# Attention probabilities turned by DMA transposes of their 16-bit halves instead of by TensorE

## The reference

```python
def dilated_group_attention(qb, kk, vv, rel_bias, window, dilation):
    ...
    s = jnp.einsum('brhnqd,brhnkd->brhnqk', qb.astype(jnp.float32), kk.astype(jnp.float32)) * scale + bias
    s = jnp.where(valid, s, NEG_INF)
    lse = jax.nn.logsumexp(s, axis=-1)
    p = jnp.exp(s - lse[..., None])
    o = jnp.einsum('brhnqk,brhnkd->brhnqd', p, vv.astype(jnp.float32))
    return o, lse

def mixer_b(xn, shared_kv, w_q, w_o, rel_bias):
    ...
    o = jnp.stack(outs, axis=0)
    lse = jnp.stack(lses, axis=0)
    wts = jax.nn.softmax(lse, axis=0)
    o = jnp.sum(wts[..., None] * o, axis=0)
    return o.reshape(b, s, D_MODEL).astype(xn.dtype) @ w_o
```

## Time and profile before

| | |
|---|---|
| median of 3 runs | 757.46 us (757.18 to 758.97) |
| the profiled execution | 759.1 us, its span 757.3 us |
| PE busy | 747.5 us, 99% of the span |
| DVE busy | 522.4 us, 69% |
| ACT busy | 420.9 us, 56% |
| POOL busy | 168.1 us, 22% |
| DMA | 144.87 MB, 191 GB/s over the span |

### The profile page before, as it was taken

One profiled execution on the slowest core, in us unless ns is written; L12 is line 12 of the kernel. 1 busy time (PEld: TensorE's weight loads), 2 busy tenths in 40 slices (PEclk: granted clock), 3 DMA queues, 4 the chain that ended last, 5 costly groups with the idle time before them and its releaser, 6 DMA issues.

```text
span 757.3 us, 13417 instructions
## 1 busy us (share of the span) xinstructions
PE 747.5 (99%) x4651; PEld 643.9 (85%) x4651; DVE 522.4 (69%) x738; ACT 420.9 (56%) x633; POOL 168.1 (22%) x298
## 2 busy tenths in 40 slices
PE   8999999999999999999999999999999999999996
PEld 7999988888888888999899898898888878888884
DVE  5788997876766657778666667568637675666653
ACT  3866667454343344866776766767746444433421
POOL 1000001225100000236656646674002000000000
PEclk9999999999999999999999999999999999999999
DMA  7745575599876575669687795696743987767602
GB/s 232 208 128 167 173 242 196 177 288 244 242 230 200 186 220 139 163 158 246 159 232 154 157 239 148 163 222 185 238 140 93 257 274 220 209 189 236 226 14 56
DMA packets 181571, 144.87 MB, mean 191 GB/s; under 512 B 29336, under 2 KB 170240, under 8 KB 181536
## 3 DMA queue, kind: packets, MB, share of 16 engines
q1 hardware_dynamic: 153344, 131.45, 55.9%
q0 software_dynamic: 6784, 7.41, 5.7%
q10 hardware_dynamic: 21408, 5.54, 5.0%
HBM read 138.02 MB, written 1.11 MB: 184 GB/s over the span
## 4 chain that ended last, share of the span: by engine, by line
PE 93%; DMA 2%; DVE 2%; issue 1%; ACT 1%; POOL 0%; DVEq 0%; POOLq 0%; SPq 0%; ACTq 0%
PE ps L1256 19%; PE ps L1257 19%; PE ps L1258 19%; PE ps L1504 10%; PE ps L1506 5%; PE ps L1262 3%; PE ps L1264 3%; PE ps L1263 3%; DMA work<-work 2%; PE ps L1567 1%; PE ps L1333 1%; PE ps L1350 1%; PE ps L1335 1%; PE ps L1336 1%; PE ps L1308 1%; PE ps L1532 1%
## 5 line engine op out<-in xcount | busy, mean ns | idle before, releaser
L841 DVE TENSOR_TENSOR w_lo<-raw,w_hi 128x2048 fp32r<-128x2048 f32 (+2 forms) x144 | 280.0, 1960 | 62.1 <-ACT w_hi L536 62.1
L536 ACT ACTIVATE w_hi<-raw 128x2048 fp32r<-128x2048 f32 (+2 forms) x144 | 233.2, 1638 | 81.5 <-DVE work L1085 29.8
L1256 PE MATMUL ps<-w_hi,xt 128*128 128x512 f32 x352 | 137.7, 391 | 0.0
L1258 PE MATMUL ps<-w_hi,xt 128*128 128x512 f32 x352 | 137.0, 389 | 0.0
L1257 PE MATMUL ps<-w_lo,xt 128*128 128x512 f32 x352 | 137.0, 389 | 0.0
L705 ACT ACTIVATE work<-ps,stat 128x256 f32<-128x256 f32 x44 | 21.0, 477 | 158.2 <-PE ps L1258 156.1
L445 POOL TENSOR_SCALAR stat<-stat 128x1 f32<-128x1 f32 x15 | 9.7, 648 | 407.4 <-ACT work L552 383.4
L1256 PE MATMUL ps<-w_hi,ot 128*128 128x512 f32 x240 | 94.9, 395 | 0.4 <-DVE ot L1106 0.4
L1257 PE MATMUL ps<-w_lo,ot 128*128 128x512 f32 x240 | 93.5, 390 | 0.0
L1258 PE MATMUL ps<-w_hi,ot 128*128 128x512 f32 x240 | 93.5, 390 | 0.0
L475 POOL DMA_DIRECT2D work<-bias_rows x128 | 71.4, 558 | 39.6 <-DVE ot L1106 25.8
(11 more groups left out here) (153 smaller groups left out, 1272.8 us busy)
## 6 DMA issues: line engine op xcount, KB each, us to landing
raw<-in_w_gate_up SPq DMA_DIRECT2D x88, 512.0 KB, 4.8
raw<-in_w_kv_b SPq DMA_DIRECT2D x96, 256.0 KB, 4.1
raw<-in_w_down SPq DMA_DIRECT2D x22, 1024.0 KB, 4.9
raw<-in_w_q_b SPq DMA_DIRECT2D x48, 256.0 KB, 4.6
raw<-in_w_qkv_a SPq DMA_DIRECT2D x23, 512.0 KB, 5.3
raw<-in_w_o_a SPq DMA_DIRECT2D x4, 1024.0 KB, 6.2
work<-bias_rows POOLq DMA_DIRECT2D x128, 32.0 KB, 3.6
raw<-in_w_o_b SPq DMA_DIRECT2D x4, 1024.0 KB, 7.0
```

The source lines that it names most:

```text
L536: act.activation(w_hi[:, s % CUT, 0:size(s)], raw[:, s % RAW, 0:size(s)], ACT.Copy).then_inc(hi_made, 1)
L841: dve.tensor_tensor(w_lo[:, c, 0:n], raw[:, s % RAW, 0:n], w_hi[:, c, 0:n].bitcast(F32), ALU.subtract).then_inc(lo_made, 1)
L1256: mm(out, xs[0], ws[0], start=start, stop=False)
L1258: return mm(out, xs[1], ws[0], start=False, stop=stop)
```

## The change

For pairs 0 to 6 TensorE no longer turns the probabilities. VectorE copies each head's block of 640 words of 32 bits apart into 1280 halves of 16 bits (`part_halves`), two DMA transposes issued by ScalarE turn them (`turn_halves`), and VectorE copies the turned halves together (`join_halves`). The second transpose is issued when the first has landed. There are three such buffers in place of two larger ones: `prob[0]`, `prob[1]` and `halves_in`. Probabilities now stand in five blocks of 128 columns, and two memsets a step clear the 64 columns that no key fills. The eighth pair is still turned by TensorE. To make room in `work`, the own band of the bias moves to the tile `ones` once that is free, and for the first two heads to `halves_in`. The diff without its lines on the eighth pair's calls and the semaphores:

```diff
@@ (layout of work)
-        TURNED = (P, P + SEQ, 0, 2 * SEQ)
-        turned = [carve(P + WS) for _ in range(2)]
-        prob = [v[:, P:P + WS] for v in turned]
...
+        prob = [carve(TP) for _ in range(2)]
+        halves_in = carve(TP)
+        turned = prob
...
-        own_band = carve(NT * RUN).rearrange("p (t n) -> p t n", t=NT)
+        early_band, own_band = (v.rearrange("p (t n) -> p t n", t=NT) for v in (halves_in[:, 0:NT * RUN], ones[:, :]))
@@ gpsimd
             stats(1)
+            pool.wait_ge(rows_done, 2)
             with pool.Fori(0, PAIRS - 1) as j:
@@ scalar
+            def turn_halves(to, parts_):
+
+                act.dma_start_transpose(to.bitcast(U16).rearrange("p (b n) -> p b n", n=P), parts_.bitcast(U16)
+                                        ).then_inc(halves_turned, 16)
@@ scalar, step_b
                 low_b(p, j, 3)
+                act.wait_ge(halves_parted, j * 4 + 2 * p)
+                act.sem_inc(turns_begun, 1)
+                turn_halves(prob[1], halves_in)
                 hi(s + 7, jj)
-                transposed_b(p - 1, j, 0)
                 low_b(p, j, 4)
-                transposed_b(p - 1, j, 1)
+                act.wait_ge(halves_turned, j * 64 + 32 * p - 16)
+                act.sem_inc(turns_begun, 1)
+                turn_halves(halves_in, prob[0])
                 hi(s + 8, jj)
@@ vector, peaks
                 dve.memset(npeak[:, 0:2], 0.0)
+                for hh in range(2):
+                    dve.memset(prob[hh][:, WB[0]:PB[1]], 0.0)
@@ vector
+            def by_half(v):
+                return v.bitcast(U16).rearrange("p (w n) -> p w n", w=2)
+
+            def by_word(v):
+                return v.bitcast(U16).rearrange("p (n w) -> p w n", w=2)
+
+            def part_halves(a, j):
+                for hh, to in enumerate((halves_in, prob[0])):
+                    h = j * 4 + 2 * a + hh
+                    dve.wait_ge(norm_made, h + 1)
+                    if hh:
+                        dve.wait_ge(halves_parted, h)
+                    dve.tensor_copy(by_half(to), by_word(prob[hh])).then_inc(halves_parted, 1)
+
+            def join_halves(a, j):
+                dve.wait_ge(halves_turned, j * 64 + 32 * a + 32)
+                for hh, found in enumerate((prob[1], halves_in)):
+                    if hh:
+                        dve.wait_ge(pt_made, j * 4 + 2 * a + 1)
+                    dve.tensor_copy(by_word(turned[hh]), by_half(found)).then_inc(pt_made, 1)
@@ vector, step_b
                 take_block(p, j, 2)
+                part_halves(p - 1, j)
                 lo(s + 5, jj)
...
                 lo(s + 8, jj)
+                join_halves(p - 1, j)
                 lo(s + 9, jj)
@@ vector, before the steps
-            for hh in range(2):
-                dve.memset(turned[hh][OWN[0]:P, 0:P], 0.0)
@@ tensor, step_b
                 wide_b(p, jj, 1, 0, 3).then_inc(block_done, 1)
-                transpose_b(a, j, 0)
                 pe.wait_ge(low_used, before + 3)
                 wide_b(p, jj, 1, 1, 2).then_inc(block_done, 1)
-                transpose_b(a, j, 1)
                 pe.wait_ge(low_used, before + 4)
                 wide_b(p, jj, 1, 2, 3)
```

More of the change, by code:

```diff
@@ L53 @@
 CUT = 6
-WORK = 6848
+WORK = 6912
 HR = P // R
@@ L58 @@
 WS = sum(WB)
+PB = (0, 2 * P)
+TP = 5 * P
 A0 = -2
@@ L201, in build @@
         vb = [v.rearrange("p (t n) -> p t n", t=NT) for v in (first, second)]
-        TURNED = (P, P + SEQ, 0, 2 * SEQ)
-        turned = [carve(P + WS) for _ in range(2)]
-        prob = [v[:, P:P + WS] for v in turned]
-        turned_own = [work[:, end[0] - (2 - hh) * (P + WS):][:, 0:4 * SEQ].rearrange("p (t x) -> p t x", t=NT)
+        prob = [carve(TP) for _ in range(2)]
+        halves_in = carve(TP)
+        turned = prob
+        turned_first = [v[:, 0:4 * P].rearrange("p (t x) -> p t x", t=NT)[:, :, 0:P] for v in turned]
+        turned_own = [work[:, end[0] - (3 - hh) * TP + P:][:, 0:6 * P].rearrange("p (t x) -> p t x", t=NT)[:, :, 0:P]
                       for hh in range(2)]
@@ L273, in build @@
             "up0_done", "silu_made", "hid_made", "ht_done", "ht_hi", "ht_made"))
+        halves_parted, halves_turned, turns_begun = (sem(n) for n in ("halves_parted", "halves_turned", "turns_begun"))
         planes_made, planes_turned, planes_joined = (sem(n) for n in (
@@ L469, in head_bias @@
                 static = isinstance(h, int)
+                own_ = early_band if static else own_band
                 if not static or h >= 1:
@@ L631, in attend_b, with transposed_b @@
                 inst.then_inc(prob_made, 1)
[L633 to L638, removed]
+            def transposed_b(hh):
+                act.wait_ge(pt_done, hh + 1)
+                act.activation(turned[hh][:, 0:4 * P], bank(4 + 2 * hh), ACT.Copy)
+                act.activation(turned[hh][:, 4 * P:TP], bank(5 + 2 * hh, 0, P), ACT.Copy).then_inc(pt_made, 1)
+            def turn_halves(to, parts_):
+                act.dma_start_transpose(to.bitcast(U16).rearrange("p (b n) -> p b n", n=P), parts_.bitcast(U16)
+                                        ).then_inc(halves_turned, 16)
             def low_b(p, j, n):
@@ L822, in _ @@
             hi(FB0)
-            transposed_b(PAIRS - 1, 0, 0)
-            transposed_b(PAIRS - 1, 0, 1)
+            transposed_b(0)
+            transposed_b(1)
             hi(FB0 + 1)
@@ L1015, in scored @@
                 return dve.tensor_tensor_reduce(
-                    out=prob[hh][:, WB[0] * t:WB[0] * t + WB[t]], in0=bank(2 + 2 * hh + t, 0, WB[t]),
+                    out=prob[hh][:, PB[t]:PB[t] + WB[t]], in0=bank(2 + 2 * hh + t, 0, WB[t]),
                     in1=bias[hh][:, WB[0] * t:WB[0] * t + WB[t]],
@@ L1042, in normalize @@
                 for t in range(NT):
-                    c, part = 2 * hh + t, prob[hh][:, WB[0] * t:WB[0] * t + WB[t]]
+                    c, part = 2 * hh + t, prob[hh][:, PB[t]:PB[t] + WB[t]]
                     inst = dve.tensor_scalar(part, part, inv[:, c:c + 1], None, ALU.mult)
                 inst.then_inc(norm_made, 1)
+            def by_half(v):
[15 more added lines that the diff above has]
+                    dve.tensor_copy(by_word(turned[hh]), by_half(found)).then_inc(pt_made, 1)
             def outputs_b(a, j):
@@ L1555, in scores_b, with transpose_b @@
                     own(t, 2).then_inc(s_done, 1)
-            def transpose_b(a, j, hh):
-                h = j * 4 + (2 * a + hh)
-                pe.wait_ge(norm_made, h + 1)
+            def transpose_b(a, hh):
+                pe.wait_ge(norm_made, 2 * a + hh + 1)
                 if hh:
[L1562 to L1568, removed]
+                    pe.wait_ge(ot_made, PAIRS + a)
+                for n in range(TP // P):
+                    inst = pe.transpose(bank(4 + 2 * hh, P * n, P), prob[hh][:, P * n:P * n + P], eye[:, :])
                 inst.then_inc(pt_done, 1)
@@ L1573, in outputs_b @@
                 pe.wait_ge(pt_made, j * 4 + 2 * a + 2)
+                pe.wait_ge(ot_made, j * 2 + (PAIRS + a))
+                tokens = bank(7, 0, SEQ).rearrange("p (t x) -> p t x", t=NT)
                 for kt in range(NT):
                     for hh in range(2):
-                        mm(bank(7, P * kt, SEQ - P * kt)[DH * hh:DH * hh + DH, :], vb[a % 2][:, kt, DH * hh:DH * hh + DH],
-                           turned[hh][:, TURNED[kt]:TURNED[kt] + SEQ - P * kt], start=kt == 0, stop=False,
+                        dims = slice(DH * hh, DH * hh + DH)
+                        mm(tokens[dims, kt:, :], vb[a % 2][:, kt, dims],
+                           turned[hh][:, 3 * P:4 * P] if kt else turned_first[hh], start=kt == 0, stop=False,
                            skip_group_check=True)
-                tokens = bank(7, 0, SEQ).rearrange("p (t x) -> p t x", t=NT)
                 for r in range(R):
@@ L1698, in _ @@
             out_proj(WOB0, PAIRS, 0, range(7), [1])
-            transpose_b(PAIRS - 1, 0, 0)
+            transpose_b(PAIRS - 1, 0)
             out_proj(WOB0, PAIRS, 1, [0])
-            transpose_b(PAIRS - 1, 0, 1)
+            transpose_b(PAIRS - 1, 1)
             out_proj(WOB0, PAIRS, 1, [1, 2])
```

6 lines of the change are left out of this document (3 added, 3 removed).

## The result

The changed kernel takes 780.19 us (median of 4 runs, 776.17 to 785.8) against 757.61 (757.18 to 758.97) before: ratio 1.0293, interval 1.0267 to 1.032. I had forecast 769.5, so the sign was right, but the rise of 22.6 us was nearly twice the 12 I gave it, and the time lies at the very top of the range I had stated, 751 to 780. The profiled execution took 781.48 us, its span 779.7, 22.4 more than before's 757.3. The changed kernel's runs also lie 9.6 us apart, before's 1.8.

The account below looks back on a forecast made before the run. The prediction took a loop of VectorE, a load and ScalarE, nearly TensorE's step, to bound the changed kernel: 12.5 + 6.6 + 1.1 + 10.9 = 31.1 us a step; +11.0 and +1.2 made 769.7, stated as 769.5, range 751 to 780.

Parts of the forecast that it names:

- The loop: From low_b 0 through VectorE's lo(s+6), the load of s+9 and ScalarE's hi(s+9) to the next low_b 0: 31.1 us; chance 0.57.
- Copies and work of the loop: VectorE from low_b 0 to the end of lo(s+6): 11.1 us plus 1.85 for two parting copies less 0.44 idle, 12.5.
- ScalarE's rest: ScalarE from the start of hi(s+9) to the next low_b 0, value_b twice and two hi back to back: 10.9 us.
- delay by the transposes: What the second DMA transpose takes from the load of s+9: between nothing and 1.75 us, taken as 1.1.
- The landing: From the end of lo(s+6) to the start of hi(s+9), the load of s+9: mean 6.6 us, before the transposes' delay.
- The period term: Six turns from low_b 0 of step 1 to that of step 7: 6 x (31.1 - 29.26) = +11.0 us.
- the end: From the last low_b 0, in step 7, to the next outputs_b: 24.2 us where before took 23.0, +1.2 us.
- a wait at the step's start alone: Sign in the profile after: if TensorE waits only at the step's start, the two transposes are the bound.
- The whole gain: Rival: TensorE stays the bound and its 7.7 us are won whole, 749.8 us; chance 0.20.
- the loop falling back to where it was: Rival: landing stays at 5.6 us, transposes take nothing from it, 29.0 to 29.3 a turn: 756 to 758.5 us; chance 0.12.
- The series of transposes: Rival: the two ordered transposes' landings, L1 + L2, bound the step from 14.9 us; with 8 each, 778; chance 0.08.
- GpSimd held by the copies: Rival: each VectorE copy holds GpSimd for its whole length, 3.7 us a step: 765.5 us; chance 0.03.

Follow-up runs that it names:

- x5: Kernel before, with two idle copies of 1280 halves put on VectorE between take_block 2 and lo(s+5) in steps 1 to 7: 759.63 us.
- x1: Changed kernel without its two DMA transposes and the waits for them, VectorE's four copies of halves kept: 760.85 us.
- x7: Changed kernel with the first of the two DMA transposes left out, the other issued at the second's place: 774.34 us.
- x9: Changed kernel without GpSimd's 24 small DMAs a step in the steps' loop (bias gathers): 773.05 us.
- x3: Changed kernel with value_b of tile 0 moved ahead of hi(s+9) in ScalarE's order, nothing left out: 779.53 us.
- x6: Changed kernel with the second of the two DMA transposes left out, only the first issued: 765.2 us.
- x2: Changed kernel with its four copies of halves a step replaced by memsets of 8 columns, both DMA transposes kept: 766.18 us.
- x8: Changed kernel with head 0 turned by one DMA transpose, head 1 by TensorE, and value_b of tile 0 ahead of hi(s+9): 758.4 us.
- x12: Changed kernel without its two DMA transposes, copies kept, and value_b of tile 0 ahead of hi(s+9): 754.19 us.

## Why the prediction was right in sign and short in size

- **The loop is what bounds the changed kernel, not TensorE.** Right. The chain runs through it, in each of steps 2 to 6 ScalarE waits for the load of s+9 by 3.9 to 4.4 us, and the rest of 10.9 us behind that wait has no idle in it. The parts make 12.2 + 9.5 + 10.9 = 32.6 us for these five turns, where 31.1 was forecast; with step 1's the mean is 32.77. The earlier trace rows with TensorE at 29.26 of 29.26 could not show it; the earlier trace rows did. x5 says how much slack it had in before: the parting copies' 1.75 us alone cost 0.35 a turn there.
- **Copies and work of the loop.** Right: 12.2 us where 12.5 was forecast. The copies took 0.826 and 0.888 us, where the earlier trace rows gave 0.915.
- **ScalarE's rest.** Right: 10.9 us.
- **The step that failed is the term "delay by the transposes".** I gave it 1.1 us, between nothing and the second one's own 1.75. The landing rose from 6.2 us (x1, same copies) to 9.5: 3.3 us. My upper end rested on the premise that a transpose takes from the load only its own engine time, taken from one transpose alone on the engines. Beside loads each added 2.6 (first) and 4.9 us (second) of engine time. By the queues the second's own packets took 1.4 us, and those of the loads 3.7 us more for each. And x7 showed that the load of s+8 was delayed as well, which the sum left out: `hi(s+8)` came 7.2 us after `lo(s+5)` where x1 has 5.1, and through `lo(s+8)` that delays the join.
- **What that makes.** The period term is 6 x (32.77 - 29.24) = 21.2 us where 11.0 was forecast. From the A of step 7 to the next step it was 22.4 us, where 24.2 was forecast, so that the end gave 0.6 us back in place of costing 1.2. The A of step 1 came 1.05 us later than before's. It lay between 339.9 and 341.5 in the kernels that are not after or x9, and why isn't settled. 21.2 - 0.6 + 1.05 = 21.7 of the 22.4 us.
- **TensorE's waits.** Before k2, by 1.1 us on average (6.6 in 6), as forecast, and at the step's start behind the joining copy, 9.9 in 6, also as forecast. I had named a wait at the step's start alone as the sign that the transposes in series bind. TensorE waited at both, so the sign didn't appear, and the wait at the start isn't much of one either: before the join VectorE waited for the DMA 3.3 us in all of after, and never in x7, where TensorE still waited 12.4 us for the join. The join is late since it stands behind `lo(s+8)`.
- **The rivals.** The whole gain is refuted, and so is the loop falling back to where it was, by the period. The series of transposes gave 778, near the measured time, for another reason than the measured one: in step 3 the first was issued at 417.45 and the joining began at 430.06, L1 + L2 of at most 12.6 us, below its threshold of 14.9; in the other six steps it was 11.7 to 14.5. In x3, with the wait for s+9 moved, it was a join behind `lo(s+8)` that bound the turns, and the transposes only the end of step 7. GpSimd held by the copies: x1, with all the copies, lands at 760.85, within 0.3 us of what the loop alone expects, and leaves it no room.
- **The hold on GpSimd itself.** The 0.1 us a copy that I read from the earlier trace rows was too small. In before an issue like the one below took 0.55 us, and in x5, beside the two idle copies, 1.89 (step 3; 1.64 to 1.75 in steps 4 to 7), so two copies held it for 1.1 to 1.3 us. In after such an issue took 0.75 to 0.93 beside a copy. GpSimd is held, more than I allowed, and had the slack for it. Before and x5:

```profile
377.80 0.55 POOL L477 DMA_DIRECT2D work<-bias_rows  x1
```

```profile
407.07 1.89 POOL L477 DMA_DIRECT2D work<-bias_rows  x1
```

- **The Trainium skill's rate** (Advanced Engine Details and Errata, X-Bar Transpose): as fast as other DMAs, 350 to 400 GB/s. No run reaches it, but x6 and x7 come nearer than the lone one's 194. By the growth of q10, a transpose of 328 KB took 1.1 us at the first place (about 300 GB/s) and 1.4 at the second (about 230), and with both in a step 2.25 each (about 146). So the rate isn't what my term lacked. With the slowed neighbours included the second cost 4.9 us of engine time.

## What to carry to other kernels

When an operation moves from the busiest engine to DMA, ask first which loop of engines and loads is nearly as long as its step: here 7.7 us of TensorE were to be saved, two engines were a third idle, and their loop through one load still set the time of the changed kernel. Price a transfer that runs beside loads on the critical path by what it does to them, not by its own time when alone; here the second transpose, issued at the moment of the loads, cost three times the first. And two costs in one loop with little slack are not additive: test each alone, and both together, before either is called cheap.

## What the runs showed of the hardware beyond that

- The same 131.45 MB of the queue of the weight loads took 55.9% of 757.3 us x 16 engines before and 57.2% of 779.7 after: 423 and 446 us. The transposes' queue went from 5.0% to 8.9%, that is 31.5 us more for fourteen, 2.25 each. The rows of after:

```profile
q1 hardware_dynamic: 153344, 131.45, 57.2%
q10 hardware_dynamic: 39776, 10.13, 8.9%
```

- That engine time alone isn't the delay: x2 has 58.2% of 768.1 us in q1, 447 us as after has, and is 14 us faster. By x6 and x7 it matters which load is beside a transpose.
- The issue of a transpose of 1280 halves took ScalarE 1.35 to 2.42 us in after (median 1.42), 4.38 at worst in x3. From issue to landing it was 3.4 to 10.1 us, median 6.4:

```profile
L647 ACTq DMA_TRANSPOSE work<-work x14: 1346/1424/2416, 350.7 to 550.8; - x14
...
DMA to landing us min/median/max: 3.4/6.4/10.1
```

- Kernels with the DMA transposes tend to vary more from run to run: 9.6 us between the extremes in after, 9.0 in x6, 7.6 in x8, 4.0 in x3; without them 4.6 in x1, 2.3 in x12. Before has 1.8 in its four runs of the comparison and 3.9 in the 26 taken beside x6. Why is open.
